# A two-layer hybrid decoder trunk in float32: one more pair of feed-forward tiles by seven products, VectorE making the token operands, gated tiles split three slabs ahead

## What is computed

```
for l in range(2):
    x = x + hybrid_mixer(x, ...)         # stick-breaking attention + retention, gated, projected
    h = rms_norm(x, ffn_norm[l])         # x: (512, 1024), float32
    a, b = split(h @ w_up[l], 2)         # 2 x 2816 columns
    a = causal_depthwise_conv3(a) + conv_b
    x = x + (silu(a) * b) @ w_down[l]
return rms_norm(x, final_norm)
```

## Time and profile before

| what | value |
|---|---|
| median of three runs | 1649.26 us |
| the profiled execution's own time | 1652.25 us |
| its span, first to last instruction | 1650.4 us |
| busy: PE, DVE, ACT, POOL | 97%, 66%, 43%, 14% |
| mean granted TensorE clock | 0.993 of full |
| DMA packets | 196.98 MB, mean 119 GB/s |

### The profile page before, as it was taken

The page is one execution under the profiler, slowest core; times in us unless marked ns, Lnnn a source line. Parts: engine busy times, 40 slices in busy tenths (PEclk is TensorE's granted clock), DMA queues, the critical chain, the costliest instruction groups (busy, mean ns, idle before and its releaser), DMA issues.

```text
span 1650.4 us, 21537 instructions
## 1 busy us (share of the span) xinstructions
PE 1607.6 (97%) x8634; PEld 1388.8 (84%) x8634; DVE 1084.7 (66%) x1191; ACT 707.2 (43%) x901; POOL 229.0 (14%) x237
## 2 busy tenths in 40 slices
PE   9999999999998999989999999999999989999898
PEld 7888888888887999967888888888888879998777
DVE  8267865775678788734262778657757887787322
ACT  5254444533345555532233533345333555555213
POOL 4000000000441122202030000000005502221020
PEclk9999999999999999999999999999999999999999
DMA  5232222122326778422333322221222268883222
GB/s 194 95 115 84 83 77 90 65 84 94 102 90 187 213 226 233 139 77 80 99 107 101 113 77 77 78 101 65 80 99 100 92 197 226 229 239 111 78 89 90
DMA packets 56253, 196.98 MB, mean 119 GB/s; under 512 B 6240, under 2 KB 6752, under 8 KB 56160
## 3 DMA queue, kind: packets, MB, share of 16 engines
q1 hardware_dynamic: 49392, 174.02, 31.1%
q0 software_dynamic: 4608, 16.78, 6.1%
q10 hardware_dynamic: 2160, 4.86, 1.0%
HBM read 191.44 MB, written 2.10 MB: 117 GB/s over the span
## 4 chain that ended last, share of the span: by engine, by line
PE 81%; DVE 7%; DMA 5%; issue 4%; ACT 2%; POOL 1%; SPq 0%; DVEq 0%; POOLq 0%; ACTq 0%
PE ps L1481 19%; PE ps L1482 19%; PE ps L1483 19%; PE ps L1487 6%; PE ps L1489 6%; PE ps L1488 6%; DMA w_raw<-wts 4%; DVE w_lo L1007 2%; DMA far_raw<-wts 1%; PE ps L1610 1%; PE ps L1599 1%; DVE cc L1169 1%; ACT w_hi L635 1%; DVE g_lo L1181 1%; PE ps L1577 1%
## 5 line engine op out<-in xcount | busy, mean ns | idle before, releaser
L1007 DVE TENSOR_TENSOR w_lo<-w_raw,w_hi 128x1024 fp32r<-128x1024 f32 x210 | 281.3, 1351 | 229.3 <-ACT w_hi L635 228.9
L1481 PE MATMUL ps<-u_hi,w_hi 128*128 128x512 f32 x832 | 326.6, 393 | 1.6 <-DVE w_lo L1007 1.6
L1483 PE MATMUL ps<-u_hi,w_lo 128*128 128x512 f32 x832 | 324.1, 390 | 0.0
L1482 PE MATMUL ps<-u_lo,w_hi 128*128 128x512 f32 x832 | 324.1, 389 | 0.0
L635 ACT ACTIVATE w_hi<-w_raw 128x1024 fp32r<-128x1024 f32 x210 | 218.8, 1054 | 237.1 <-DMA w_raw<-wts 230.5
L1481 PEld LDWEIGHTS ps<-u_hi,w_hi 128*128 128x128 f32 x832 | 156.4, 188 | 33.4 <-DVE w_lo L1007 2.5
L1483 PEld LDWEIGHTS ps<-u_hi,w_lo 128*128 128x128 f32 x832 | 156.2, 188 | 33.1
L1482 PEld LDWEIGHTS ps<-u_lo,w_hi 128*128 128x128 f32 x832 | 156.4, 188 | 30.6
L1487 PE MATMUL ps<-comb_hi,far_hi 128*128 128x256 f32 x512 | 147.2, 288 | 7.9 <-issue 7.6
L1488 PE MATMUL ps<-comb_lo,far_hi 128*128 128x256 f32 x512 | 146.5, 286 | 0.0
L1481 PE MATMUL ps<-g_hi,w_hi 128*128 128x512 f32 x264 | 105.9, 401 | 21.7 <-DVE g_lo L1181 21.7
(11 more groups left out here) (262 smaller groups left out, 3236.9 us busy)
## 6 DMA issues: line engine op xcount, KB each, us to landing
w_raw<-wts SPq DMA_DIRECT2D x258, 512.0 KB, 3.3
far_raw<-wts SPq DMA_DIRECT2D x56, 512.0 KB, 4.7
w_raw<-wts POOLq DMA_DIRECT2D x16, 512.0 KB, 6.0
far_raw<-wts POOLq DMA_DIRECT2D x16, 512.0 KB, 7.1
w_odd<-wts SPq DMA_DIRECT2D x8, 512.0 KB, 6.1
q<-q ACTq DMA_DIRECT2D x8, 256.0 KB, 3.5
xs<-xt SPq DMA_DIRECT2D x7, 256.0 KB, 6.0
out<-rows SPq DMA_DIRECT2D x7, 256.0 KB, 2.3
```

The costliest lines, as they stand in the source:

```text
L1007: nc.vector.tensor_tensor(w_lo[:, s, :], w_raw[:, s, :], w_hi[:, s, :].bitcast(F32), ALU.subtract).then_inc(s_lo, 1)
L1481: nc.tensor.matmul(dst, a_hi, b_hi, start=start, stop=False)
L1482: nc.tensor.matmul(dst, a_hi, b_lo, start=False, stop=False)
L1483: return nc.tensor.matmul(dst, a_lo, b_hi, start=False, stop=stop)
```

## The change

- PLAIN goes from 3 to 2: a layer has 8 plain slabs and 9 iterations.
- The eight sums and scalings of the token operands go from POOL (`combine` is deleted, its call too) to VectorE (`normed`, `combined`). ScalarE writes the gain operands in two calls of eight, one ahead of `root`.
- Part 1 alternates between two ring slots, 0 and 3, with two semaphores, and its load and its accumulating DMA are issued an iteration earlier than they were.
- For iteration 0 the parts 3 to 6 are loaded to a new `first_raw`, in the memory of `g_raw`'s tiles 14 to 21.
- Gated pairs 0 to 2 are split in the last iteration, and pair c at slab c-3, ahead of that slab's weights.
- ScalarE's and VectorE's lists in the plain slabs and in iteration 0 are written anew; in iteration 0 TensorE waits for the last plain bank before product 1.

```diff
-PLAIN = 3
+PLAIN = 2
 PAIRS = FT // 2
 SPLIT = PAIRS - PLAIN
 DOWN0 = UP0 + 4 * PLAIN
...
+        first_raw = sb("first_raw", [P, 4, SLAB], F32, M + 28 * K)
...
-        s_sum1 = sem("s_sum1")
+        s_el1 = [sem(f"s_el1{b}") for b in range(2)]
+        s_sum1 = [sem(f"s_sum1{b}") for b in range(2)]
...
-                return w_raw[:, ring(l, k), :]
+                return w_raw[:, ring(l, (1, 3 * (n % 2), 2)[k]), :]
+            if n == 0:
+                return first_raw[:, k - 3, :]
             if k < 6:
                 return far_raw[:, k - 3, :]
-            return w_odd[:, ring(l, 2), :] if n % 2 == 0 else far_raw[:, 3, :]
+            return w_odd[:, ring(l, 2), :] if n % 2 == 1 else far_raw[:, 3, :]
...
+                return w_lo[:, ring(l, (1, 3 * (n % 2), 2)[k]), :]
...
+            return w_hi[:, ring(l, 2), :] if n % 2 == 1 else far_lo[:, 3, :]
...
-                return w_hi[:, ring(l, k), :]
+                return w_hi[:, ring(l, 1 - k), :]
...
                 base = l * SLABS + DOWN0 - RING + SLOT_CREDIT
                 sp.wait_ge(s_free, base + 1)
+                load_part(l, 0, 1, W11, s_el1[0])
+                load_part(l, 0, 4, W12, s_el[4])
+                load_part(l, 0, 3, W21, s_el[3])
+                sp.wait_ge(s_free, base + 2)
                 load_part(l, 0, 0, W11, s_el[0])
-                sp.wait_ge(s_free, base + 2)
-                load_part(l, 0, 1, W11, s_el[1])
+                load_part(l, 0, 5, W22, s_el[5])
                 sp.wait_ge(s_free, base + 3)
                 load_part(l, 0, 2, W22, s_el[2])
                 load_part(l, 0, 6, W21, s_el6[0])
                 sp.wait_ge(s_free, base + 4)
-                load_part(l, 0, 3, W21, s_el[3])
-                load_part(l, 0, 4, W12, s_el[4])
-                load_part(l, 0, 5, W22, s_el[5])
+                load_part(l, 1, 1, W11, s_el1[1])
                 for n in range(SPLIT):
                     done = 7 * (l * SPLIT + n)
                     more = n + 1 < SPLIT
@@ -480,18 +485,15 @@
                     if more:
                         load_part(l, n + 1, 0, W11, s_el[0])
                     else:
+                        sp.wait_ge(s_prod, done + 2)
                         load(ring(l, 0), l * SLABS + DOWN0)
-                    sp.wait_ge(s_prod, done + 2)
-                    if more:
-                        load_part(l, n + 1, 1, W11, s_el[1])
-                    else:
                         load(ring(l, 1), l * SLABS + DOWN0 + 1)
+                    if n + 2 < SPLIT:
+                        sp.wait_ge(s_prod, done + 2)
+                        load_part(l, n + 2, 1, W11, s_el1[n % 2])
                     sp.wait_ge(s_prod, done + 3)
                     if more:
                         load_part(l, n + 1, 2, W22, s_el[2])
-                    else:
-                        load(ring(l, 2), l * SLABS + DOWN0 + 2)
-                    if more:
                         sp.wait_ge(s_prod, done + 4)
                         load_part(l, n + 1, 3, W21, s_el[3])
                         sp.wait_ge(s_prod, done + 5)
@@ -499,6 +501,7 @@
                         sp.wait_ge(s_prod, done + 6)
                         load_part(l, n + 1, 5, W22, s_el[5])
                     else:
+                        load(ring(l, 2), l * SLABS + DOWN0 + 2)
                         sp.wait_ge(s_prod, done + 7)
                         load(ring(l, 3), l * SLABS + DOWN0 + 3)
...
-            def combine(l):
...
+                        split_hi(l, i + AHEAD)
+                    if j == 0:
+                        with_gain(l, (5, 6))
+                    if j == 1:
+                        plain_tap(l, 0, 0)
+                    if j == 3:
+                        silu(l, 0)
+                        plain_tap(l, 0, 1)
+                    if j == 4:
+                        comb_high(l, 0)
+                        silu(l, 1)
+                        comb_high(l, 1)
+                    if j == 5:
+                        comb_high(l, 2)
+                        comb_high(l, 3)
+                        plain_tap(l, 1, 0)
+                    if j == 6:
+                        part_high(l, 0, 0)
+                        silu(l, 2)
+                    if j == 7:
+                        part_high(l, 0, 1)
+                        for k in range(4, 7):
                             comb_high(l, k)
...
-                            if k == 1:
-                                gated_high(l, 0)
+                            gated_high(l, k)
                 for i in range(DOWN0, SLABS):
+                    c = i - DOWN0 + 3
+                    if c < PAIRS:
+                        gated_high(l, c)
                     if i == DOWN0:
                         last_quarter(l, SPLIT - 1)
                         for h in range(2):
                             tap(l, SPLIT - 1, h)
                     if i + AHEAD < SLABS:
                         split_hi(l, i + AHEAD)
-                    if i - DOWN0 + 1 < PAIRS:
-                        gated_high(l, i - DOWN0 + 1)
-                    if i == DOWN0:
+                    if i == DOWN0 + 1:
                         for h in range(2):
                             silu(l, FT - 2 + h)
...
+            def normed(l, tile, half, gains):
+
+                row = rinv[:, half * 256:half * 256 + 256].rearrange("p (a t) -> p a t", a=1).broadcast_to([P, 4, S // 2])
+                dve.wait_ge(s_xgain, l * 16 + gains)
+                dve.wait_ge(s_r, l * 3 + 3)
+                nc.vector.tensor_tensor(tile[:], tile[:], row, ALU.mult).then_inc(s_v, 1)
...
+                if which == 1:
+                    nc.vector.tensor_tensor(s1[:], a22[:], late2[:], ALU.subtract).then_inc(s_comb, 1)
+                if which == 2:
+                    nc.vector.tensor_tensor(s3[:], late2[:], a11[:], ALU.subtract).then_inc(s_comb, 1)
+                if which == 3:
+                    dve.wait_ge(s_comb, l * 4 + 1)
+                    nc.vector.tensor_tensor(s5[:], s1[:], a11[:], ALU.add).then_inc(s_comb, 1)
+                if which == 4:
+                    dve.wait_ge(s_comb, l * 4 + 3)
+                    nc.vector.tensor_tensor(s4[:], s5[:], a12[:], ALU.subtract).then_inc(s_comb, 1)
...
+                        if (g, j) == (0, 0):
+                            normed(l, comb[0], 0, 4)
+                            normed(l, comb[3], 0, 8)
+                        if (g, j) == (0, 1):
+                            plain_out(l, g, 0)
+                            normed(l, late2, 1, 12)
+                            normed(l, comb[6], 1, 16)
+                            combined(l, 1)
+                        if (g, j) == (0, 2):
+                            combined(l, 2)
+                            combined(l, 3)
+                            conv(l, 0)
+                        if (g, j) == (0, 3):
+                            plain_out(l, g, 1)
+                            combined(l, 4)
+                            plain_gated(l, 0)
+                        if (g, j) == (1, 0):
+                            conv(l, 1)
+                            comb_low(l, 0)
+                            plain_gated(l, 1)
+                            comb_low(l, 1)
+                        if (g, j) == (1, 1):
+                            plain_out(l, g, 0)
+                            comb_low(l, 2)
+                            conv(l, 2)
+                        if (g, j) == (1, 2):
+                            comb_low(l, 3)
                             part_low(l, 0, 0)
-                        elif i + AHEAD == DOWN0 + 2:
+                            plain_gated(l, 2)
+                        if (g, j) == (1, 3):
                             third_sum(l, 0)
-                            fourth_sum(l, 0)
                             part_low(l, 0, 1)
...
+                    if n == 0:
+                        fourth_sum(l, 0)
                     part_low(l, n, 2)
...
+                    else:
+                        comb_low(l, 4)
                     part_low(l, n, 3)
+                    if n == 0:
+                        comb_low(l, 5)
+                        part_low(l, n, 4)
+                        comb_low(l, 6)
                     conv(l, 2 * (PLAIN + n) - 1)
-                    part_low(l, n, 4)
+                    if n > 0:
+                        part_low(l, n, 4)
...
+                        gated_low(l, 0)
                         split_lo(l, DOWN0 + 1)
-                        gated_low(l, 0)
...
+                        gated_low(l, 1)
                         split_lo(l, DOWN0 + 2)
+                        gated_low(l, 2)
                 for i in range(DOWN0, SLABS):
+                    c = i - DOWN0 + 3
+                    if c < PAIRS:
+                        gated_low(l, c)
+                    if i == DOWN0:
+                        conv(l, FT - 2)
                     if i + AHEAD < SLABS:
                         split_lo(l, i + AHEAD)
```

(9 more changed lines are left out.)

91 lines of the change are left out of this document (25 added, 66 removed).

## The result

Each set of runs with its median, lowest and highest time in us:

| kernel | median | lowest | highest | runs | ratio to the kernel before, 95% interval |
|---|---|---|---|---|---|
| before, beside it | 1650.51 | 1648.46 | 1652.29 | 4 | |
| changed | 1606.95 | 1602.43 | 1607.72 | 4 | 0.9731 [0.9708, 0.9754] |

A forecast was written before the change was run, and what follows sets the result against it. PE, busy 97% of the span, was taken as the bound, leaving less streaming or fewer pauses; 3.4 + 29.8 + 10.4 + 2.0 + 3.6 = 49.2 us off gave 1603.0 or 1600.1, forecast 1601.5, range 1595.5 to 1615.

The forecast's parts named there:

- The down slabs: First eleven down slabs of each layer: splitting gated pairs earlier ends the g_lo waits and half-clock stretches, -29.8 us.
- The entry: Start of each layer's iterations: early loads into first_raw shorten the first iteration, 2.5 us a layer staying; -10.4 us.
- The working on DVE up to the last bank: Before product 1: DVE works without idle until 499.6 us, product 1 being due at 497.6.
- The slack of the loads: At the entry: part 2 lands 4.3 us after its slab, with 5.4 us left, so no transfer is last.
- After it DVE has two or three operations for each 2.86 us product and keeps up: First iteration after product 1: DVE keeps pace, so no further wait was charged beyond 2.5 us a layer.
- Rival A: At the entry the pause halves the clock again, a 3.4 us stretch costing 1.7 a layer: 1605 us; chance 0.15.
- Rival B: DVE enters the iterations so late that the old excess stays, none of 10.4 us returning: 1612 us; chance 0.10.
- C: Down slabs still wait, for something else, and half of the pauses stay: 1616 us; chance 0.04.
- D: In the iterations transfers become the bound and the kernel gets slower: 1666 us, chance 0.03; small form 1610, chance 0.06.
- The high end of the range: Old entry excess kept (1612 us) plus 3 us for the iterations' excess kept: 1615 us.
- Plain slabs: Plain slabs: with POOL idle there and slabs split early in DVE's list, -2.0 us.
- later iterations: Iterations after the first: product 1's wait goes, POOL's g_raw and part 4's sum leave 1.5 us a layer; -3.6 us.

The follow-up runs named there:

- e1: Kernel before with only the gated pairs split three slabs ahead; median 1623.59 us, ratio 0.9845.
- e2: Changed kernel with gated pairs split behind the weights again, one slab ahead; median 1634.15 us, ratio 0.9916.
- e8: Changed kernel without first_raw, parts 3 to 6 of iteration 0 loaded when the last plain slab is done; median 1622.18 us.
- e4: e3 with VectorE's comb_low(3) and plain_gated(2) also moved behind the last plain banks; median 1605.37 us.
- e3: Changed kernel with ScalarE's silu of the last plain tile moved behind copy_u in iteration 0; median 1602.37 us.
- e7: Changed kernel with one slot for part 1, its load and sum one iteration later; median 1610.47 us.
- e10: e5 with iteration 0's part 6 loaded where part 5 was, part 5 last, and VectorE's comb_low(3) moved behind the banks; median 1603.77 us.
- e6: Changed kernel with the eight scalings and sums of the token operands back on POOL; median 1615.87 us.
- e5: Changed kernel with all silus behind copy_u and, in iteration 0, VectorE's part_low(1, 0) behind the subtraction of copy_y; median 1601.77 us.

## Why the prediction was right, and where it was not

**The down slabs** were right in mechanism and place: no wait for g_lo, eleven slabs in 59.9 us, clock 1.00. By the profile the term came out at 30.0 for 29.8. By medians e1 and e2 give 25.6 and 27.2, so for the median the term was 3 to 4 us too large. It was read from an execution 3.0 us above the median, and I took it whole.

**The entry** is the step that failed in size: 6.4 us came back of the 10.4. One reading under it was wrong. The text says that product 2 of the kernel before starts 3.79 us late for the loads of parts 3 to 5; DVE's rows above and e8 show that it waited for DVE's block of comb_lo. The change removes that block too, so the wait went all the same, for a reason that the prediction doesn't give. The working on DVE up to the last bank was right. It is busy without a pause, its last bank is taken at 500.59, which less the late start of 1.7 us is 498.9 against 499.6 in the text, and product 1 is 1.4 and 1.6 us late, for cb on DVE, inside the 1.0 to 2.0 given. The slack of the loads was read too large: the text gives part 2's load 4.3 us of 5.4, the median of the iterations, and at the entry of e4 it took 6.1 (issued at 489.52, summed from 495.65). What was missed stands in the sentence "After it DVE has two or three operations for each 2.86 us product and keeps up". DVE did keep up with the products, but I followed only DVE's list. The taps come last in it, ACT's silu waits for the taps, copy_u stands behind the silu, and product 4 is 2.0 us late in each layer. e3 shows it: with that silu moved, this wait goes. So 1.4 + 2.0 us were left in layer 1 and 1.6 + 2.0 in layer 2, where I had 2.5 a layer; with small delays the two make 3.6, and 5.4 with the 1.6 us of a half-clock stretch in layer 2.

**Rival A** came true in part, at 0.15. A half-clock stretch of 3.4 us stands in layer 2 at 1306.4, behind the two pauses of 1.37 and 1.84 us, and not in layer 1 behind pauses of 1.13 and 1.85. The other runs show that the length of such pauses doesn't decide it: the clock stayed at 1.00 in layer 2 of e2 behind 1.98 and 1.85 us, and in layer 1 of e7 behind 2.08 and 1.84, and fell in layer 1 of e2 (1.44 and 1.85) and of e10 (1.80 alone). Around each pause of 3.8 us or more, in both layers of the kernel before, e1, e6 and e8, it fell. The Trainium skill (TensorE: Matmul & The Clock Gate, HAM oscillation) describes waits for transfers after each of which PE goes on at half rate. It speaks of waits longer than the 1.1 to 2.1 us here; those of 3.8 us and more agree with it. What decides for the shorter ones stays open. The only execution with a mean clock of 1.000 took 1602.43 us, near the forecast. A's time was 1605, the median is 1606.95.

**Rival B** did not come, nor did C or D. No wait of PE is put down to a transfer. The high end of the range adds 3 to B's 1612, while the ends that the text gives for the other iterations (3.5 a layer for 1.5) would add 4; nothing hangs on it.

**Plain slabs and later iterations** were right in size, 2.1 for 2.0 and 3.8 for 3.6. Of the latter the mechanism was half right. The wait before product 1 went, as said; what stays is not put down to POOL's g_raw or part 4's sum, as the text has it, but again to copy_u behind the silus: product 4 is 0.5 to 0.8 us late in four of sixteen iterations. e5 took these waits away. Whether POOL's g_raw lies behind them, by slowing the taps that the silus wait for, was not tested.

**The late start** of the profiled execution, 1.7 us, was nowhere in the working. With 4.0 for the entry it gives 1608.7 from 1603.0, the forecast on the profile's own scale; small differences of the other stages take off 1.0, to 1607.72.

## What to carry to other kernels

When work moves from one engine to another, go through the lists of the engines that wait for the receiver as well. An operation that frees a bank should not stand behind one that waits for the busiest engine, since it inherits that wait (here 2 us a layer, gone by moving one silu, though half of it came back at a later product). Where an engine is full up to a due time, look for the next limit before taking work off it: here the loads had the same date, and a lighter list made the first iterations longer in e4 and in e10. And where a trace gives "issue" as the reason of a wait, compare the start with the ends on the other engines before you name a cause.
